# Splitting the turning of an expert's token rows by block: the second block of 128 rows is turned at the start of the two-block branch

## The reference, cut to what matters

```python
gate = (group_gate[:, :, None] * inner_gate[:, None, :]).reshape(b * s, N_EXPERTS)
for e in range(N_EXPERTS):
    a, u = jnp.split(t @ w_ei[e], 2, axis=-1)        # 1024 -> 2 x 512
    y = y + gate[:, e:e + 1] * ((jax.nn.silu(a) * u) @ w_eo[e])   # 512 -> 1024
return layer_norm(ALPHA * x + moe, ln2_g, ln2_b)
```

## Time and profile before

| what | us |
|---|---|
| median of 3 runs | 1334.46 (1333.02 to 1336.57) |
| the profiled execution, its own time | 1336.53 |
| its span, first to last instruction | 1334.9 |
| TensorE busy in the span | 1255.9 (94%) |
| VectorE busy | 702.0 (53%) |
| ScalarE busy | 622.2 (47%) |
| GpSimd busy | 352.0 (26%) |

### The profile page before, as it was taken

The page is one execution under the profiler, slowest core; times in us unless marked ns, Lnnn a source line. Parts: engine busy times, 40 slices in busy tenths (PEclk is TensorE's granted clock), DMA queues, the critical chain, the costliest instruction groups (busy, mean ns, idle before and its releaser), DMA issues.

```text
span 1334.9 us, 19105 instructions
## 1 busy us (share of the span) xinstructions
PE 1255.9 (94%) x7182; PEld 1032.6 (77%) x7183; DVE 702.0 (53%) x890; ACT 622.2 (47%) x844; POOL 352.0 (26%) x306
## 2 busy tenths in 40 slices
PE   5999999999999999999999999589999999989992
PEld 4888866788878888966788878467788888868871
DVE  4233367422476333267522365867854765785456
ACT  4222367532233322366632230757744665775445
POOL 0532000000120332000000030157643756575333
PEclk9999999999999999999999999689999999999997
DMA  6742100023363322200022544479977978898653
GB/s 220 249 155 95 64 1 1 32 95 122 130 231 116 126 95 95 96 1 1 1 96 84 186 153 177 131 265 293 342 252 217 299 241 299 264 341 280 179 182 154
DMA packets 63522, 212.33 MB, mean 159 GB/s; under 512 B 12391, under 2 KB 12903, under 8 KB 62648
## 3 DMA queue, kind: packets, MB, share of 16 engines
q1 hardware_dynamic: 49052, 178.24, 38.7%
q0 software_dynamic: 11808, 24.59, 7.1%
q10 hardware_dynamic: 2592, 8.53, 1.6%
HBM read 199.00 MB, written 34.25 MB: 175 GB/s over the span
## 4 chain that ended last, share of the span: by engine, by line
PE 84%; DVE 5%; ACT 3%; DMA 3%; issue 2%; POOL 2%; SPq 0%; POOLq 0%; DVEq 0%; ACTq 0%
PE banks L737 23%; PE banks L738 22%; PE banks L739 22%; PE banks L846 3%; PE banks L882 2%; PE banks L917 2%; PE banks L1037 2%; PE banks L924 2%; DMA x_rows<-x_rows,slot_tab 1%; PE banks L857 1%; PE banks L771 1%; DMA moe_raw<-in_expert_w 1%; POOL gated L607 1%; DVE moe_lo L1476 1%; ACT moe_hi L1324 1%
## 5 line engine op out<-in xcount | busy, mean ns | idle before, releaser
L1495 DVE TENSOR_TENSOR wlo<-raw,whi 128x2048 fp32r<-128x2048 f32 (+1 forms) x52 | 116.0, 2231 | 176.6 <-ACT whi L1153 176.6
L1476 DVE TENSOR_TENSOR moe_lo<-moe_raw,moe_hi 128x2048 fp32r<-128x2048 f32 x81 | 183.6, 2287 | 32.2 <-ACT moe_hi L1324 31.6
L1324 ACT ACTIVATE moe_hi<-moe_raw 128x2048 fp32r<-128x2048 f32 x96 | 182.9, 1916 | 30.9 <-PE banks L739 17.1
L737 PE MATMUL banks<-xT,whi 128*128 128x512 f32 x448 | 176.0, 393 | 0.0
L738 PE MATMUL banks<-xT,whi 128*128 128x512 f32 x448 | 175.5, 392 | 0.0
L739 PE MATMUL banks<-xT,wlo 128*128 128x512 f32 x448 | 175.4, 391 | 0.0
L607 POOL TENSOR_TENSOR gated<-gated,kqv 128x512 f32<-128x512 f32 x16 | 25.3, 1596 | 489.9 <-DVE kqv L1640 489.9
L737 PE MATMUL banks<-moe_lo,xeh 128*128 128x512 f32 x368 | 146.7, 399 | 5.9 <-DVE moe_lo L1476 4.2
L737 PE MATMUL banks<-wlo,xT 128*128 128x256 f32 (+1 forms) x448 | 136.0, 304 | 13.2 <-DVE wlo L1495 13.2
L738 PE MATMUL banks<-moe_hi,xeh 128*128 128x512 f32 x368 | 144.7, 393 | 0.0
L739 PE MATMUL banks<-moe_hi,xel 128*128 128x512 f32 x368 | 144.7, 393 | 0.0
(11 more groups left out here) (273 smaller groups left out, 2324.2 us busy)
## 6 DMA issues: line engine op xcount, KB each, us to landing
moe_raw<-in_expert_w SPq DMA_DIRECT2D x192, 512.0 KB, 5.9
raw<-in_front_w SPq DMA_DIRECT2D x104, 512.0 KB, 4.9
toeplitz_rows<-bias_rows POOLq DMA_DIRECT2D x4, 1152.0 KB, 13.5
kqv<-in_x_turned SPq DMA_DIRECT2D x8, 512.0 KB, 7.6
pt<-in_x SPq DMA_DIRECT2D x2, 2048.0 KB, 10.2
x_rows<-pt ACTq DMA_DIRECT2D x8, 512.0 KB, 2.7
token_sums<-pt ACTq DMA_DIRECT2D x8, 512.0 KB, 3.7
moe_raw<-token_sums SPq DMA_DIRECT2D x8, 512.0 KB, 8.0
```

Source lines behind the costliest of these rows:

```text
L737: mm(dst, left[0], right[1], start=first, stop=False)
L1324: A(moe_hi[m % SPLIT_E], moe_raw[m % RAW_E], ACT.Copy).then_inc(e_hi, 1)
L1476: V.tensor_tensor(moe_lo[m % SPLIT_E], moe_raw[m % RAW_E], moe_hi[m % SPLIT_E].bitcast(F32), ALU.subtract).then_inc(lo_sem(m % ECH), 1)
L1495: V.tensor_tensor(view(lo, shape), view(raw[c % 2], shape), view(hi, shape).bitcast(F32), ALU.subtract).then_inc(w_split, 1)
```

## The change

The four groups of an expert's rows are cut by block instead of by column piece: a group is now four 128-column pieces of one block, called (block, half). The two groups of block 0 are still turned during the expert before, both among the matmuls of c4 (`row_of_next(0)`, `row_of_next(1)`); the call after c2 is gone. The two groups of block 1 are turned only in the two-block branch, at its beginning. In the one-block branch a matmul of c0 raises the counter `rows_T` in their place, because the other engines still copy whatever is in those banks. c0 on block 0 now waits only for the first turned group, and c0 on block 1 for all four. ScalarE and VectorE copy the groups of block 1 after the two `y_sb` copies and before chunk c5. The gathers of the two blocks get counters of their own, and the turns of expert 0 need only the gather of block 0.

```diff
-FIRST_BANKS = (2, 3, 6, 7)
+ROW_BANKS = ((2, 3), (1, 3))
@@ GpSimd, gathers
-                        oob_is_err=False).then_inc(rows_in[b], 16)
+                        oob_is_err=False).then_inc((rows0_in, rows1_in)[c][b], 16)
@@ TensorE
+            def turn_rows(b, c, g):
+                tb = bank[ROW_BANKS[c][g]]
+                for q in range(4):
+                    k = 4 * g + q
+                    last = nc.tensor.transpose(tb[:, q * P:(q + 1) * P], x_rows[b][:, c * D + k * P:c * D + (k + 1) * P], ident)
+                last.then_inc(rows_T, 1)
+            pe.wait_ge(rows0_in[0], 16)
+            for g in range(2):
+                turn_rows(0, 0, g)
             def step(pair, b, width, more=True):
-                pe.wait_ge(xe_lo, z * 4 + 4 + 2)
+                if width > P:
+                    pe.wait_ge(rows1_in[b], pair * 16 + 16)
+                    turn_rows(b, 1, 0)
+                    pe.wait_ge(xe_lo, z * 4 + 2 + 2)
+                    turn_rows(b, 1, 1)
+                def row_of_next(g):
+                    if more:
+                        pe.wait_ge(rows0_in[1 - b], pair * 16 + (16 if b == 0 else 32))
+                        if g == 1:
+                            pe.wait_ge(xe_lo, z * 4 + 2 + 4)
+                        turn_rows(1 - b, 0, g)
+                for c in range(2):
+                    pe.wait_ge(lo_sem(c), lo_by(z, c))
+                    pe.wait_ge(xe_lo, z * 4 + 2 + c + 1)
+                    last = in_part(c, 0)
+                    if width > P:
+                        pe.wait_ge(xe_lo, z * 4 + 2 + 4)
+                        last = in_part(c, 1)
+                    last.then_inc(e_used, 1)
...
                     if c == 2:
                         turn_acts(0)
-                        rows_of_next(0, 1)
...
-                rows_of_next(2)
+                row_of_next(0)
                 turn_acts(1)
...
-                rows_of_next(3)
+                row_of_next(1)
@@ ScalarE, expert (VectorE the same with row_lo)
-                rows_hi(1 - b, z + 1, (0, 1))
...
-                rows_hi(1 - b, z + 1, (2,))
+                row_hi(1 - b, z + 1, 0, 0)
                 acts_hi(z, 1)
-                rows_hi(1 - b, z + 1, (3,))
+                row_hi(1 - b, z + 1, 0, 1)
...
                 for d in range(2):
                     A(y_sb[b][:, d * 512:(d + 1) * 512], bank[4 + d][:, :], ACT.Copy, scale=slot_gate(b, 0)).then_inc(y_act, 1)
+                for g in range(2):
+                    row_hi(1 - b, z + 1, 1, g)
                 e_split(pair, b * ECH + XCH + 1 + SPLIT_E)
```

More of the change, by code:

```diff
@@ L424, in encoder_kernel @@
         y_gone = sem("y_gone")
-        rows_in = [sem(f"rows_in{i}") for i in range(2)]
+        rows0_in = [sem(f"rows0_in{i}") for i in range(2)]
+        rows1_in = [sem(f"rows1_in{i}") for i in range(2)]
         rows_T, xe_hi, xe_lo = sem("rows_T"), sem("xe_hi"), sem("xe_lo")
@@ new lines, in in_part @@
+                def in_part(c, r):
+                    n, half, kh = b * ECH + c, c // 2, c % 2
+                    w = [t[n % SPLIT_E].rearrange("p (k n) -> p k n", k=KD // 2) for t in (moe_hi, moe_lo)]
+                    for k in range(KD // 2):
+                        last = mm3(bank[2 - 2 * half + r][:, :], [v[:, kh * (KD // 2) + k, r * P:(r + 1) * P] for v in xv],
+                                   [v[:, k] for v in w], kh == 0 and k == 0, kh == 1 and k == KD // 2 - 1)
+                        if width == P and c == 0 and k == 0:
+                            last.then_inc(rows_T, 2)
+                    return last
@@ L1074, in step @@
                     for r in range(width // P):
-                        for k in range(KD // 2):
-                            last = mm3(bank[2 - 2 * half + r][:, :], [v[:, kh * (KD // 2) + k, r * P:(r + 1) * P] for v in xv],
-                                       [v[:, k] for v in w], kh == 0 and k == 0, kh == 1 and k == KD // 2 - 1)
+                        last = in_part(c, r)
                     last.then_inc(e_used, 1)
@@ L1338, in _, with row_hi @@
             act.wait_ge(logit_ready, NT + 2)
[L1340 to L1343, removed]
+            def row_hi(b, z, c, g):
+                if (c, g) == (1, 1):
+                    act.wait_ge(xe_lo, z * 4 + 2 + 2)
+                act.wait_ge(rows_T, z * 4 + 2 * c + g + 1 + 8)
+                A(row_part(xe[b][0], c, g), turned_part(c, g), ACT.Copy).then_inc(xe_hi, 1)
             for c in range(EARLY_E, RAW_E + 1):
@@ L1364, in _ @@
                 e_split(0, c)
-            rows_hi(0, 0, range(4), FIRST_BANKS)
+            for c in range(2):
+                for g in range(2):
+                    row_hi(0, 0, c, g)
             act.wait_ge(counted, 1)
@@ L1368, in gated_half @@
             def gated_half(z, half):
+                if half == 0:
+                    act.wait_ge(xe_lo, z * 4 + 2 + 4)
                 act.wait_ge(e_used, SPLIT_E + z * ECH + 2 * half + 2)
@@ L1858, in _, with row_lo @@
             V.tensor_copy(n_pass[:, 0:1], most).then_inc(counted, 1)
[L1860 to L1864, removed]
+            def row_lo(b, z, c, g):
+                dve.wait_ge(xe_hi, z * 4 + 2 * c + g + 1)
+                V.tensor_tensor(row_part(xe[b][1], c, g), turned_part(c, g), row_part(xe[b][0], c, g).bitcast(F32),
+                                ALU.subtract).then_inc(xe_lo, 1)
             for c in range(2, SPLIT_E):
                 e_split(0, c)
-            rows_lo(0, 0, range(4), FIRST_BANKS)
+            for c in range(2):
+                for g in range(2):
+                    row_lo(0, 0, c, g)
             dve.wait_ge(counted, 1)
@@ L1871, in _ @@
             dve.wait_ge(slots_out, 32)
-            dve.wait_ge(rows_in[1], 32)
+            dve.wait_ge(rows0_in[1], 16)
+            dve.wait_ge(rows1_in[1], 16)
             def gated_half(z, half):
@@ L1903, in expert @@
                                     ALU.mult).then_inc(y_dve, 1)
+                for g in range(2):
+                    row_lo(1 - b, z + 1, 1, g)
                 e_split(pair, b * ECH + XCH + 1 + SPLIT_E)
```

41 lines of the change are left out of this document (16 added, 25 removed).

## The result

| kernel | median us | runs | profiled execution | its span |
|---|---|---|---|---|
| before | 1335.25 | 4 (1333.02 to 1336.57) | 1336.53 | 1334.9 |
| after | 1361.56 | 4 (1357.69 to 1366.66) | 1362.96 | 1361.3 |

The ratio is 1.0198, with a 95% interval of 1.018 to 1.0215: the change costs 26 us. Forecast were 1357.9 us and +23.4. The runs of after spread over 9 us, those of before over 3.6; the likely reason comes with experiment 6.

What follows compares the result with a forecast made beforehand. TensorE was taken to bound two-block experts and VectorE's chain one-block ones. The terms -4.8 + 5.6 + 15.2 + 0 + 5.1 + 2.3 gave +23.4 us, 1357.9 us, with an 8-in-10 range of 1343 to 1366.

Steps and rivals of the forecast that it cites:

- Turns after c2 gone: Eight transposes fewer after c2: 0.80 us saved in each of six two-block steps, nothing in nine one-block steps; -4.8 us.
- Turns at the top: The same eight transposes return before c0 in each of 7 two-block steps, 0.80 us each; +5.6 us.
- The new wait: In four two-block steps after one-block ones, c0 on block 1 waits for VectorE's late low part; +15.2 us.
- Two-block after two-block: Three such steps: VectorE's copies are ready before TensorE arrives, so the wait is hidden; 0, at worst 0.3 us each.
- The clock: Behind three of the four stalls TensorE runs a stretch at 1.2 GHz, 1.7 us each; +5.1 us, bounds 0 and 6.8.
- The variant in which the turns make all four lose it: Transposes not counting as busy, turns before each stall lengthen the pause; all four stretches lost, sum 1.7 us higher.
- The late copies: Block 1 copies behind the result copies delay experts 3, 11, 12 and 6, 8, 10; +2.3 us, bounds 0 and 8.
- The start: Expert 0 can begin some 3 us sooner, but VectorE's first product still waits for expert 1's gathers; 0, at most -1.
- rival C: Code loading at the loop's first branches: both pauses go with their lost clock, 1350, or two more come, 1365; chance 0.08.
- Rival A: TensorE's work sets the time throughout, so 72 fewer transposes give -7.2 us and the early start maybe -1: 1326.5; chance 0.08.
- Rival B: VectorE gets ahead by the 1.28 us of copies it loses; four stalls total 10.1 us, sum +15.6: 1350; chance 0.15.
- Rival D: Late copies also delay weight loads, adding up over runs of one-block experts: +6 more, 1364; chance 0.07.

Runs made afterwards that it cites:

- experiment 6: The after kernel with 8 unused identity transposes added after c2 in the one-block branch only (the run e8): 1360.61 us, ratio 1.0185.
- e2: The before kernel with 6 of the 8 transposes after c2 left out, in two-block steps only: 1331.42 us, ratio 0.9963.
- e1: The before kernel with 6 of the 8 transposes after c2 left out, in the nine one-block steps only: 1336.28 us, ratio 1.0001.
- e7: The after kernel with 12 extra unused matmuls in the two-block branch before the wait for block 1's last group: 1363.81 us, ratio 1.0207.
- e3: The after kernel with c0 and c1 both on block 0 first, so 24 matmuls and not 12 precede the wait: 1342.81 us, ratio 1.0056.
- e4: The after kernel with ScalarE's and VectorE's copies of block 1 put ahead of the two result copies: 1361.69 us, ratio 1.0193.
- e8: The after kernel with 8 unused identity transposes after c2 in the one-block branch, restoring its old length: 1360.61 us, ratio 1.0185.
- e5: e3 with VectorE making the low part of the first hidden half before the split of c1: 1340.9 us, ratio 1.0039.
- e6: The before kernel with VectorE making the low part of the first hidden half before the split of c1: 1335.16 us, ratio 0.9994.

## Why the prediction was right

1. Turns after c2 gone, -4.8 us from two-block steps and nothing from one-block steps. Right in both parts: e2 and e1. Steps 5 and 14, which give up 8 turns and get 8, are within 0.04 us of before.
2. Turns at the top, +5.6. Right: 0.79 us each, and step 15, which gets them and gives none, is 0.83 longer.
3. The new wait, +15.2. Right in mechanism and place, 2.5 us too large: the four waits lengthen the start-to-start times by 12.7. VectorE's result copies behind expert 6 began 4.36 us after the last matmul and not 5.04, behind experts 8 and 12 4.49 and not 5.04 and 4.86. Behind expert 6 it was ScalarE's wait for the weights of c4, 1.09 us in before and 0.44 in after; in e7 it is 1.37, so it differs from one execution to the next. The rest is about 0.2 us a place in the handover and the arrival. e3 settles it against the rivals, since the same copies with 2.73 us more of cover take 18.8 us off.
4. Two-block after two-block, 0. Right.
5. The clock, +5.1. The steps 4, 7, 9 and 13 grew by 20.5, of which 12.7 are waits, so 7.8 is the clock's. Three of four places lost it, as taken; that count was luck, since it was two in e4 and a different three in e8. The variant in which the turns make all four lose it came in none of them. In two of the three the stretch was 6.8 us long and cost about 2.9, not 1.7. The price was taken from a single kind of row, the short one, and the bound of 6.8 was too low.
6. The late copies, +2.3: measured +0.9 in experts 6, 8, 10 (forecast 1.0) and +1.8 in 3, 11, 12 (1.3). Expert 11's first product started without idle time, as said, 1.21 us later in its step than before, and the step grew by 1.05. Expert 12's 0.69 is not the copies' alone: a half-clock stretch lies in it that before does not have the earlier trace rows, so the forecast of the copies is borne out in size only roughly.

```profile
1214.80:1218.10 3.30, 3.30 (x12) 2.73 (x11) 0.40 (x1) 1.02 (x2) 3.26 (x2) 0.50 1.03 405
```

7. The start, 0. Right: expert 0's first matmul comes 2.67 us sooner and its last 0.14. In before VectorE's product starts 0.41 us after the last gather of expert 1 has landed (879.80) and 0.30 after the SiLU's end. In after, TensorE's first matmul, the SiLU and VectorE's product, against the earlier trace rows, and then the clock behind that first matmul (columns as in the earlier trace rows):

```profile
870.85 0.79 PE L749 MATMUL banks<-moe_lo,xeh 128*128 128x512 f32 x1 [5.35 <-DVE xel L1897]
879.44 0.60 ACT L1404 ACTIVATE silu<-banks 128x512 f32<-128x512 f32 x1 [1.05 <-PE banks L751]
880.07 0.69 DVE L1913 TENSOR_TENSOR h_full<-silu,banks 128x512 f32<-128x512 f32 x1 [5.62 <-ACT silu L1404]
```

```profile
870.85:874.15 3.30, 3.30 (x8) 2.62 (x9) 1.53 (x3) 1.08 (x2) 2.99 (x6) 0.50 1.04 420
```

So in this one execution the SiLU was last, and with it TensorE: it had paused for 5.35 us and ran its first 14 matmuls at 1.2 GHz, 0.43 us apart, which used up the early start. But the gather had landed only at 879.44, so without that it would have held the product until about 879.9 (an estimate, with the 0.41 us of before), 0.2 us sooner than it came. e3, with the same turning of expert 0, has the SiLU done at 879.03 and shows the gather as the one waited for; it landed at 880.14:

```profile
880.57 0.69 DVE L1915 TENSOR_TENSOR h_full<-silu,banks 128x512 f32<-128x512 f32 x1 [6.32 <-DMA x_rows<-x_rows,slot_tab]
```

8. The waits at the branches were in no term of the sum, only in rival C. They added 2.5 us in the profiled execution. Steps 1 and 2 last 48.8 us together there and 43.5 in e7, which has the same one-block branch, so 2.5 us is within what they vary by, and rival C is neither borne out nor excluded.

Rival A (TensorE's work sets the time) falls with e1 and e8. Rival B (VectorE gets ahead by the 1.28 us of copies it loses) is not borne out: in expert 6 of after, VectorE idles for ScalarE's high part before c3 as it did before, 1.11 us. The waits came out between its 10.1 us and the forecast 15.2, but for the reasons under 3. Rival D (weight loads, with a delay that adds up over the one-block experts) was not what after lost: steps 3, 11 and 12 grew by 1.8 us in sum. Late weight chunks are real all the same, and decided e4 and e5.

So the mechanism and the place of the main terms were right. That the sum of 23.4 came within 3 us of the 26.3 is partly luck, since larger errors cancelled: the wait was forecast 2.5 us too large, the clock 2.7 too small, and the branches' 2.5 us stood nowhere.

## What to carry to other kernels

Work taken from the busiest engine is worth its length only where that engine really sets the pace. In this matmul stream a wait of up to 0.16 us shows as no idle time (the modelled length of 0.39 us less the pace of 0.23), and two chains can end level without any wait, so compare the end of the producer with the start of the consumer in each kind of step, here 0.15 us apart. When a copy is moved behind other work of an in-order engine, add up what stands before it at the moment the consumer arrives, separately for each kind of step that can come before and not on average; then see how much independent work the consumer can do first, since 12 matmuls against 24 was worth 19 us here.

## What the runs showed of the hardware that was not expected

- The same pause of 2.8 us before expert 4 was followed by full clock in after and by some 3.4 us at 1.2 GHz in e8. Pauses of 3.1 us had stretches of 6.8 us at 1.2 GHz with them in after, one of 3.45 us had none in e4.
- At the two branches of the loop's first passes TensorE's sequencer takes up to 5.6 us for its branch instruction, later on 0.4 at most. It differs between executions: steps 1 and 2 last 46.2 us together in before, 48.8 in after, 49.7 in e8, 43.5 in e7 and 44.9 in e6.
